# A state-space scan inside a fused decoder step: its masked sums as two products of rounded parts, its start and end regrouped

## What is computed

```python
acum = jnp.cumsum(dtr * A, axis=2)                      # dta summed in a chunk
xdt = xr * dtr[..., None]
seg = acum[:, :, :, None] - acum[:, :, None, :]         # 128 x 128 per head
decay = jnp.where(causal, jnp.exp(jnp.where(causal, seg, 0.0)), 0.0)
scores = jnp.einsum('bclgn,bcsgn->bclsg', Cr, Br)[..., None] * decay
y_diag = jnp.einsum('bclsgr,bcsgrp->bclgrp', scores, xdt)
to_end = jnp.exp(acum[:, :, -1:] - acum)
states = jnp.einsum('bcsgn,bcsgr,bcsgrp->bcgrpn', Br, to_end, xdt)
chunk_decay = jnp.exp(acum[:, :, -1])
h_last, h_in = lax.scan(lambda h, i: (h * i[1][..., None, None] + i[0], h), h0, (states, chunk_decay))
y_off = jnp.einsum('bclgn,bcgrpn,bclgr->bclgrp', Cr, h_in, jnp.exp(acum))
y = y_diag + y_off + d_skip * xs                        # then * silu(z), grouped RMSNorm
```

## Time and profile before

| | us |
|---|---|
| median of 3 runs | 1758.57 (1757.16 to 1761.01) |
| the profiled execution, its own time | 1760.02 |
| its span in the trace | 1758.2 |
| stage_ssd in it: first instruction to the next stage's first | 555.8 to 645.5 |

### The profile page before, as it was taken

One profiled execution on the slowest core, in us unless ns is written; L12 is line 12 of the kernel. 1 busy time (PEld: TensorE's weight loads), 2 busy tenths in 40 slices (PEclk: granted clock), 3 DMA queues, 4 the chain that ended last, 5 costly groups with the idle time before them and its releaser, 6 DMA issues. The chain is left out here.

```text
span 1758.2 us, 32849 instructions
## 1 busy us (share of the span) xinstructions
PE 1669.6 (95%) x11957; PEld 1434.0 (82%) x11957; DVE 1148.0 (65%) x2529; ACT 762.8 (43%) x1585; POOL 432.1 (25%) x548
## 2 busy tenths in 40 slices
PE   5999999799998989998987998999999999999999
PEld 5999999689887666655655877999999999977887
DVE  6632247666766555556464368887778887687885
ACT  6322453677774235456443234322322332365342
POOL 1321110666775543334352001000000000040000
PEclk9999999799999989999998999999999999999999
DMA  5533211120101247547593232322222332593343
GB/s 162 99 107 108 53 43 26 25 50 21 25 16 29 65 143 272 192 142 272 173 398 136 73 97 65 116 91 97 90 90 94 107 112 84 176 381 96 94 120 108
DMA packets 158858, 204.24 MB, mean 116 GB/s; under 512 B 55110, under 2 KB 109423, under 8 KB 158674
## 3 DMA queue, kind: packets, MB, share of 16 engines
q1 hardware_dynamic: 136058, 121.66, 23.2%
q0 software_dynamic: 22368, 80.46, 12.9%
q10 hardware_dynamic: 312, 0.52, 0.1%
HBM read 164.69 MB, written 37.90 MB: 115 GB/s over the span
## 5 line engine op out<-in xcount | busy, mean ns | idle before, releaser
L2977 PE MATMUL banks<-u_sum,w_sum 128*128 128x264 f32 x2904 | 358.4, 285 | 3.4 <-DVE w_sum L3008 3.4
L2977 PEld LDWEIGHTS banks<-u_sum,w_sum 128*128 128x128 f32 x2904 | 355.7, 189 | 4.1 <-DVE w_sum L3008 4.0
L470 PE MATMUL banks<-u_parts_mix,w_in_parts 128*128 128x352 f32 x1440 | 243.5, 326 | 4.4 <-DVE u_parts_mix L838 4.4
L470 PEld LDWEIGHTS banks<-u_parts_mix,w_in_parts 128*128 128x128 f32 x1440 | 230.7, 189 | 7.8 <-DVE u_parts_mix L838 4.8
L1982 PE MATMUL banks<-turned,cmp_w 128*128 128x512 f32 x256 | 133.4, 603 | 4.7 <-DVE turned L2109 3.0
L2107 ACT ACTIVATE turned<-banks 128x512 f32<-128x512 f32 (+1 forms) x136 | 78.7, 587 | 125.8 <-PE banks L1970 125.5
L3316 PE MATMUL banks<-wd_hi,gd_hi 128*128 128x512 f32 x308 | 120.2, 390 | 1.4 <-DVE gd_lo L3347 1.0
L3316 PE MATMUL banks<-wd_lo,gd_hi 128*128 128x512 f32 x308 | 120.0, 390 | 0.0
L3316 PE MATMUL banks<-wd_hi,gd_lo 128*128 128x512 f32 x308 | 119.9, 389 | 0.0
L1970 PEld LDWEIGHTS banks<-consts,rows_grouped 128*128 128x128 f32 x512 | 64.7, 144 | 66.7 <-issue 57.2
L3204 POOL DMA_DIRECT2D rest_whole<-g_rest x1 | 0.6, 594 | 466.3 <-issue 466.3
(11 more groups left out here) (459 smaller groups left out, 3340.1 us busy)
## 6 DMA issues: line engine op xcount, KB each, us to landing
gd_whole<-g_sums SPq DMA_DIRECT2D x77, 256.0 KB, 2.7
g_sums<-silu_gate SPq DMA_DIRECT2D x55, 256.0 KB, 2.1
w_gate_raw<-in_w_gate SPq DMA_DIRECT2D x11, 1024.0 KB, 5.4
w_up_raw<-in_w_up SPq DMA_DIRECT2D x11, 1024.0 KB, 5.4
w<-in_w_down POOLq DMA_DIRECT2D x33, 256.0 KB, 18.4
w_in_raw<-in_w_in SPq DMA_DIRECT2D x29, 256.0 KB, 3.4
g_sums<-s SPq DMA_DIRECT2D x22, 256.0 KB, 2.3
x_tile<-in_x_prompt SPq DMA_DIRECT2D x8, 512.0 KB, 4.1
```

The source lines that it names most:

```text
L470: mm = nc.tensor.matmul(bank[:, 0:PIECE], w[:, pb, :], u[:, pa, k, tokens(p)], start=(k == 0 and (pa, pb) == TERMS[0]), stop=(k == KT - 1 ...
L2977: mm = nc.tensor.matmul(bank(tg, i), wp[side, p][:, a, k, :], m.u[tg, i, b][:, k, :], start=(k == 0 and (a, b) == TERMS[0]), stop=(k == kh ...
```

## The change

**The sums of masked steps.** dta is split once, by DVE at the stage's start, into a rounded part (HI, type fp32r) and the rest (LO, also rounded): `parts`. `td` gets a second plane: POOL fills the HI plane as before (its output is fp32r now), ACT fills the LO plane with eight copies of the mask, one for each head, scaled per row by that head's LO part (`low_steps`). `strict` becomes fp32r too. PE then makes each masked sum as two fp32r products that add up in PSUM, instead of one float32 product.

**The start.** POOL's clearing of `cpad` is gone. ACT copies C into `cpad`, DVE clears the two halves that stay zero, after the split of dta.

**The end.** DVE gates the last tile itself (`last_gated`), ACT copies out the last state before it squares the last tile, and the four stores of the prompt's state move into SP's queue of the next stage, behind its first loads.

**The gathers.** `EARLY` goes from 9 to 7, since the second plane takes the memory of two ring blocks: two gathers move from the scan to the start of POOL's gathers in the sample attention.

```diff
+    hout = m.hout = sb("state_out", [P, DB + 1, 2, NG, HD])
+    td = sb("dt_steps", [P, 2, 2, 8, P], F32R)
+    parts = sb("dta_parts", [P, 2, NT + 1, 8], F32R)
...
                     pe.wait_ge(s.td_ready, i + 1)
+                    pe.wait_ge(s.td_low, i + 1)
                     for h in range(2):
                         if i >= 1:
                             pe.wait_ge(s.e_ready, 2 * (i - 1) + h + 1)
-                        nc.tensor.matmul(m.bank[SEG0 + h][0:r, 0:4 * r], strict(i), td[0:r, i % 2, 4 * h:4 * h + 4, 0:r],
-                                         start=True, stop=True).then_inc(s.seg_ready, 1)
+                        for part in (HI, LO):
+                            x = nc.tensor.matmul(m.bank[SEG0 + h][0:r, 0:4 * r], strict(i), td[0:r, i % 2, part, 4 * h:4 * h + 4, 0:r],
+                                                 start=part == HI, stop=part == LO)
+                        x.then_inc(s.seg_ready, 1)
...
+                def low_steps(i):
+                    r = rows[i]
+                    if i >= 2:
+                        act.wait_ge(s.seg_ready, 2 * (i - 1))
+                    for h in range(8):
+                        x = nc.scalar.activation(td[0:r, i % 2, LO, h, 0:r], tri(i), ACT.Copy,
+                                                 scale=parts[0:r, LO, tile[i], h:h + 1].bitcast(F32))
+                    x.then_inc(s.td_low, 1)
...
+                for g in range(NG):
+                    h = slice(64 * g, 64 * g + 64)
+                    x = nc.scalar.activation(cpad[h, g, :], m.xc[h, 5, :], ACT.Copy)
+                x.then_inc(s.cpad_ready, 1)
+                act.wait_ge(s.parts_ready, 1)
+                low_steps(0)
+                low_steps(1)
                 act.wait_ge(s.sums_taken, 1)
...
                     if i < n:
                         exps(i)
+                    if i + 2 < n:
+                        low_steps(i + 2)
                     if i >= 3:
                         take_out(i - 3)
...
                 take_out(DB - 1)
+                take_out(DB)
                 square(n - 1)
-                take_out(DB)
...
-                nc.gpsimd.memset(cpad[:, :, :], 0.0).then_inc(s.padded, 1)
+                pool.wait_ge(s.parts_ready, 1)
                 steps(0)
...
-                    if i >= 1:
+                    if 1 <= i < n:
                         gate(i - 1)
...
                 def prologue():
+                    for r, tiles in ((P, slice(0, NT)), (NS, slice(NT, NT + 1))):
+                        dta = m.dt[0:r, tiles, 8:16]
+                        chain(nc.vector.tensor_copy(parts[0:r, HI, tiles, :], dta))
+                        i = nc.vector.tensor_tensor(parts[0:r, LO, tiles, :], dta, parts[0:r, HI, tiles, :].bitcast(F32), ALU.subtract)
+                    i.then_inc(s.parts_ready, 1)
...
-                    dve.wait_ge(s.padded, 1)
                     for g in range(NG):
-                        h = slice(64 * g, 64 * g + 64)
-                        i = nc.vector.tensor_copy(cpad[h, g, :], m.xc[h, 5, :])
-                    i.then_inc(s.cpad_ready, 1)
+                        i = nc.vector.memset(cpad[64 * (1 - g):64 * (1 - g) + 64, g, :], 0.0)
+                    i.then_inc(s.padded, 1)
                     dve.wait_ge(s.sums_ready, 1)
...
+                    if i == n - 1:
+                        dve.wait_ge(s.y_taken, n)
+                        nc.vector.tensor_tensor(out(i), out(i), m.z[0:r, tile[i], :], ALU.mult).then_inc(s.last_gated, 1)
...
-                sp.wait_ge(s.out_taken, DB + 1)
-                for i in range(4):
-                    sp.dma_start(hd(io.p_ssm)[:, 0, i, :], hout[:, DB, i % 2, i // 2, :]).then_inc(m.ssd_stored, 16)
...
-RING, EARLY = 12, 9
+RING, EARLY = 12, 7
...
                 load_values(0)
+                for i in range(4):
+                    sp.dma_start(by_head_pair(io.p_ssm)[:, 0, i, :], m.hout[:, DB, i % 2, i // 2, :]).then_inc(m.ssd_stored, 16)
```

20 lines of the change are left out of this document (11 added, 9 removed).

## The result

The changed kernel takes **1750.2 us** in the median of six runs (1746.77 to 1753.25), the kernel before 1758.38 in the median of six runs beside them; the ratio is 0.9949, interval 0.9937 to 0.9960. Forecast were 1749.5 us and 9.1 us less; measured are 8.2 less. Five later runs gave 1749.91 and a ratio of 0.9961 (0.9947 to 0.9974), so 8.2 to 8.5 us less. The profiled execution of the changed kernel took 1746.77 us, span 1745.0. It is the lowest of the six, and the 13.2 us by which its span lies under before's 1758.2 are more than the change brings in the median.

What follows compares the result with a forecast made beforehand. PE's queue alone was taken to bound the loop, but not the stage's start and end. 5.6 + 1.0 + 2.5 = 9.1 us off the median 1758.57 gave 1749.5 us, range 1745.5 to 1754.

Steps and rivals of the forecast that it cites:

- Part 1, the sums: Scan loop: fp32r masked sums take 0.80 us per tile off PE's queue, over tiles 2 to 8: 5.6 us.
- the lower of the two bounds: Loop, POOL's rounded HI-plane product: taken as 1.91 us, with 2.94 from the nearest rounded row as the other bound.
- another engine takes over: Rival: ACT's copies or POOL's rounded product hold the loop period near 7.5, part 1 brings 2.0, 1753 us; chance 13%.
- Part 2, the start: Stage's start: PE restarts 2.3 us earlier, less 1.3 for the clock: 1.0 us (from -1.4 to 3.6).
- the 1.25 taken: Stage's start: assumed time in us for each DVE clearing of 1056 columns on 64 rows.
- The clock's loss of 1.3: Stage's start: PE runs partly at the lower clock after its restart, losing 1.3 us more than now.
- the 2.2 that I gave as the worst: Stage's start: worst clock loss, 4.4 us at half speed after PE's restart, 2.2 us.
- the 5 us that I had named as a sign of being wrong: Sign against the forecast: a clock staying low for more than 5 us after PE's restart.
- Part 3, the end: Stage's end: the stage ends at about 642.0 instead of 644.61 and the next starts at 643.0: 2.5 us.
- Part 4, the gathers: Next stage's start: the moved gathers of blocks 7 and 8 land in time and cost nothing.
- the clock stays up: Rival: clock stays up at the start or rises earlier in the next stage, up to 1.3 and 2.2 more, 1747.5; 15%.

## Why the prediction was right, point by point

**Part 1, the sums (5.6 us).** Right. The period is 6.99 for 6.98, and T to E is 59.09 - 53.60 = 5.49 us shorter, of which undoing the sums gives back 5.48. The four products show 1.17 where 1.08 was forecast, but only because the first row begins 0.08 early; what the queue loses is 0.79, for 0.80. PE was and is the bound: leaving products out shortens the turn, doubling ACT's work does not lengthen it. ACT's copies were mis-sized upwards: they start every 0.29 us (2.44 for eight) instead of 0.39, and ACT is busy 4.6 instead of 5.6 us. POOL's rounded product takes 1.91, the lower of the two bounds. The sum rested on neither. The rival "another engine takes over" needed copies of 0.6 us.

**Part 2, the start (1.0 us).** Its terms are right in size, the reason behind one of them is not. DVE's copies of the sums end 6.91 - 4.59 = 2.3 us earlier relative to S, as forecast. But the 4.27 us of the copies of C were mostly waiting for POOL's operations, as the rows of the start show, and not the work of copying; that clearings of this shape are free of it was not foreseen, and in this the 2.3 is in part luck. One clearing takes 0.94 with 0.26 of issue behind the one before it, near the 1.25 taken; the 1.1 us by the Trainium skill (VectorE: DVE Perf Modes, section Zero memsets can be issued as uint32) was 0.16 too long for the operation alone. PE's restart comes 2.05 earlier. DVE reaches `b_of_b` 2.43 earlier (9.14 us after S for 11.57), and it takes 1.75 where it took 1.36 before, because POOL's product beside it now waits for ACT's exponentials, behind the low planes. The sum had no term for this. The clock's loss of 1.3 could not be read from the profile of the changed kernel, which had none, and by that profile this step looked wrong. Five profiles with this start give 0, 0.73, 1.35, 2.48 and 2.82, in the mean 1.5, against 0.25 of the kernel before: some 1.2 more. So the 1.3 holds as a mean. What I had not seen is that it is a spread and no value. Two of the five lie beyond the 2.2 that I gave as the worst, and in them the clock stayed low for 5.2 and 5.9 us behind the restart, more than the 5 us that I had named as a sign of being wrong; in the other three the sign did not show. Nor had I seen that POOL's clearing would hold up the split of dta by 1.7 us if it stayed: with the start undone T comes 0.8 us later than in the kernel before, so moving it was needed for the sums to bring their full gain.

**Part 3, the end (2.5 us).** Right, slightly low: 6.23 - 3.51 = 2.72, and undone it gives back 2.72. ACT ends at 633.76 and the next stage begins 0.9 later, as taken; DVE's gating took its 0.7.

**Part 4, the gathers (0).** Right: 1.0004 for that edit alone, and the earlier trace rows's copy, which first needs block 7, has no wait in the changed kernel:

```profile
648.31 1.30 DVE L2247 COPY rows_grouped<-cache_ring 128x1024 f32<-128x1024 f32 x2
```

**The sum.** From S to N the two profiles differ by 89.71 - 79.16 = 10.55 us, with the clock up at the start after; less the mean clock loss of 1.5 us after (before's 0.25 is in the 10.55 already) that is 9.1, against 9.1 forecast and 8.2 to 8.5 measured. In the profiled pair another 2.4 us lie behind N (1112.7 against 1110.3). Nearly all of that is in stages that the change does not touch. PE's work at the lower clock there is shorter in that execution: behind N + 20 us PE was busy for 24.7 us at the lower level before and for 17.6 after. In the other profiles without added products the part behind N lasts from 1110.4 to 1114.2 us. So this part is the execution's, not the change's.

Undoing the three parts one at a time costs 4.0 + 4.8 + 4.2 = 13.0 us in the medians, more than the 8.2 of the whole. In the profiles it is 5.2 + 3.2 + 2.7 = 11.1 against 10.55, and the 0.5 between them is the hold-up of the split (0.8) less the low parts' cost at the start (0.3), which each alone doesn't show. The rest of the difference is not placed; each median is known to about 2 us either way.

Of the rivals, "the clock stays up" is half of what the first profile shows (1746.8): at the start the clock was up at the restart, at the seam it stayed low until 5.7 us after N, and N to F is 19.30 against 19.48. In the medians it does not show.

## What to carry to other kernels

Where one engine has no gap over a whole loop, what its queue loses comes off the time to the hundredth, and the other engines can take new work up to the period, and in a short loop a little over it, if it is made turns ahead. At the places where the bounding engine restarts after a pause, read several profiles before you believe a difference of 1 to 3 us: the clock's level there belongs to the execution. When work is put on an engine at a stage's start, look at what its neighbour does in the same microseconds, not at the engine's own row alone: a VectorE row that is long beside a GpSimd row may be waiting, though the profile shows it as busy.

## What the runs showed of the hardware

- A rounding copy of 128x64 on VectorE took 1.87 us beside a clearing of 128x2112 on GpSimd (two profiles), and 0.20 without it.
- A VectorE copy of 64x1056 that ran into a GpSimd product of 128x1024 ended 0.56 to 0.57 us after it, whatever its start (2.69 and 3.66 us long, four profiles); VectorE clearings of the same shape beside the same product took 0.94.
- A VectorE product of 32x1024 took 1.07 to 1.09 us plus its overlap with such a GpSimd product (13 profiles).
- ScalarE's scaled copies of 128 columns start every 0.29 us, though each lasts about 0.39; eight take 2.44.
- Clearing 1056 columns on 64 rows took VectorE 0.94 us in every profile that has it, with 1.19 between two starts.
- Four rounded products of 512 columns took 1.17 us among other work, 0.23 between starts, and two fewer saved 0.46 a turn; the float32 instructions that they replace start 0.43 apart.
- The granted clock fell in one execution and not in another of the same program at the same place; products that compute nothing kept it up over a seam in two of two profiles and brought 1.3 us there; with six instead of four of them behind the seam, and no products at the start, it fell in the one profile taken.
